# The forgetting term of the attention scores, from four-row matmuls to matmuls over all 128 rows

## The reference

```
log_f  = log_sigmoid(fc + b_f)              # 512 frames x 4 heads
F      = cumsum(log_f, over frames)
logits = (q @ k.T) * 64**-0.5 + F[query] - F[key]   # per head
p      = softmax(logits where key <= query)
out    = p @ v
```

## Time and profile before

| | us |
|---|---|
| median of 3 runs (lowest to highest) | 1547.85 (1547.56 to 1548.93) |
| the profiled execution, its own time | 1548.7 |
| its span | 1546.9 |
| TensorE matmuls busy | 1521.0 (98%) |
| VectorE busy | 1013.9 (66%) |
| ScalarE busy | 703.6 (45%) |

### The profile page before, as it was taken

How to read it: one execution, slowest core, us unless ns; L and a number is a source line. 1 busy time by engine, 2 the same in 40 slices (tenths; PEclk the granted TensorE clock), 3 DMA queues, 4 the chain that set the end, 5 groups by cost and what they waited for, 6 DMA issues and landing times.

```text
span 1546.9 us, 20345 instructions
## 1 busy us (share of the span) xinstructions
PE 1521.0 (98%) x7184; PEld 1232.9 (80%) x7184; DVE 1013.9 (66%) x1818; ACT 703.6 (45%) x1214; POOL 49.9 (3%) x39
## 2 busy tenths in 40 slices
PE   7899999999999999999999999999999999999997
PEld 5677877788888888888877788777888888888886
DVE  5778765556587743777468787655656777357754
ACT  5666554433444422443376565433434443234434
POOL 0000000000300000000110000000021000000011
PEclk9999999999999999999999999999999999999999
DMA  6222212223232223332432112122323332333232
GB/s 225 69 68 69 69 62 69 68 87 111 86 105 95 86 92 113 98 102 68 124 122 82 67 57 80 57 69 75 94 84 118 98 104 73 104 109 96 80 92 74
DMA packets 43862, 139.27 MB, mean 90 GB/s; under 512 B 5508, under 2 KB 5636, under 8 KB 43528
## 3 DMA queue, kind: packets, MB, share of 16 engines
q1 hardware_dynamic: 43344, 137.45, 28.3%
q10 hardware_dynamic: 440, 0.80, 0.2%
HBM read 136.13 MB, written 2.10 MB: 89 GB/s over the span
## 4 chain that ended last, share of the span: by engine, by line
PE 92%; DVE 3%; ACT 3%; issue 1%; DMA 0%; SPq 0%; DVEq 0%; ACTq 0%
PE dense L565 28%; PE dense L567 27%; PE dense L566 27%; PE branch L625 2%; PE turned L610 2%; PE scores L596 1%; PE scores L597 1%; PE scores L600 1%; ACT tmp L919 1%; DVE wlo L1066 0%; DMA h<-in_x 0%; ACT whi L792 0%; DVE act L1146 0%; DVE act L1143 0%; PE dense L778 0%
## 5 line engine op out<-in xcount | busy, mean ns | idle before, releaser
L565 PE MATMUL dense<-hg,whi 128*128 128x512 f32 x1376 | 552.2, 401 | 13.4 <-DVE wlo L1080 9.0
L567 PE MATMUL dense<-hg,wlo 128*128 128x512 f32 x1376 | 538.8, 392 | 0.0
L566 PE MATMUL dense<-hg,whi 128*128 128x512 f32 x1376 | 538.2, 391 | 0.0
L792 ACT ACTIVATE whi<-raw 128x1024 fp32r<-128x1024 f32 (+3 forms) x275 | 266.6, 969 | 451.6 <-PE dense L567 450.7
L1066 DVE TENSOR_TENSOR wlo<-raw,whi 128x1024 fp32r<-128x1024 f32 (+3 forms) x275 | 306.7, 1115 | 169.6 <-ACT whi L792 166.5
L565 PEld LDWEIGHTS dense<-hg,whi 128*128 128x128 f32 x1376 | 259.8, 189 | 76.8 <-issue 10.7
L567 PEld LDWEIGHTS dense<-hg,wlo 128*128 128x128 f32 x1376 | 259.4, 189 | 55.9
L566 PEld LDWEIGHTS dense<-hg,whi 128*128 128x128 f32 x1376 | 260.0, 189 | 50.6 <-issue 0.7
L565 PE MATMUL dense<-act,whi 128*128 128x512 f32 x608 | 239.2, 393 | 0.0
L567 PE MATMUL dense<-act,wlo 128*128 128x512 f32 x608 | 236.8, 390 | 0.0
L566 PE MATMUL dense<-act,whi 128*128 128x512 f32 x608 | 236.7, 389 | 0.0
(11 more groups left out here) (136 smaller groups left out, 1240.6 us busy)
## 6 DMA issues: line engine op xcount, KB each, us to landing
raw<-in_w_up SPq DMA_DIRECT2D x88, 512.0 KB, 3.5
raw<-in_w_gate SPq DMA_DIRECT2D x48, 512.0 KB, 3.5
raw<-in_w_in SPq DMA_DIRECT2D x35, 512.0 KB, 3.5
raw<-in_w_down SPq DMA_DIRECT2D x32, 384.0 KB, 3.0
raw<-in_w_down SPq DMA_DIRECT2D x32, 320.0 KB, 2.9
raw<-in_w_out SPq DMA_DIRECT2D x16, 512.0 KB, 3.5
raw<-in_w_br_a SPq DMA_DIRECT2D x8, 512.0 KB, 3.5
h<-in_x SPq DMA_DIRECT2D x8, 256.0 KB, 6.6
```

The costliest lines, as they stand in the source:

```text
L565: mm(out, a, xhi, start=start, stop=False)
L566: mm(out, a, xlo, start=False, stop=False)
L567: return mm(out, b, xhi, start=False, stop=stop)
L792: fn(whi[:, s, 0:cols], raw[:, r, 0:cols], ACT.Copy).then_inc(w_hi.sem, 1)
```

## The change

`f_rows` is replaced by two tiles. `fk` (128 x 512) is the key's side as before, all heads in one tile. `fq` (128 x 4 x 512) is the query's side, once for each head f: the sum of before, multiplied by `own_rows[:, f]`, which is 1 on rows 32f to 32f+31 and 0 elsewhere. The third matmul of a C step takes all 128 rows of both. So ahead of unit 15 VectorE has five instructions where it had two: four for `fq` (with two operands that are columns) and one for `fk`. The constants grow by four columns, and the program is built with `dynamic_dma_scratch_size=1024`.

```diff
+    parts["own_rows"] = np.arange(P)[:, None] // 32 == np.arange(4)[None, :]
...
-                  ("spread1", 2), ("eps", 1)):
+                  ("spread1", 2), ("own_rows", 4), ("eps", 1)):
...
-        f_rows = sb("f_rows", [P, 2, S], F32R)
+        fq = sb("fq", [P, 4, S], F32R)
+        fk = sb("fk", [P, S], F32R)
...
                 if forget:
-                    f = 32 * (2 * (p - A_PAIRS - B_PAIRS) + s)
-                    last = mm(b[:, 0:n], f_rows[f:f + 4, 0, t * P:(t + 1) * P], f_rows[f:f + 4, 1, 0:n],
-                              start=False, stop=True)
+                    f = 2 * (p - A_PAIRS - B_PAIRS) + s
+                    last = mm(b[:, 0:n], fq[:, f, t * P:(t + 1) * P], fk[:, 0:n], start=False, stop=True)
...
                         dve.wait_ge(group.sem, group.at(l, c))
-                        ve.tensor_scalar(f_rows[:, c, :], bank[g % 4][:, :], spread1[:, c:c + 1], None,
-                                         ALU.add).then_inc(aug.sem, 1)
+                        if c == 0:
+                            for f in range(4):
+                                last = ve.tensor_scalar(fq[:, f, :], bank[g % 4][:, :], spread1[:, 0:1],
+                                                        own_rows[:, f:f + 1], ALU.add, ALU.mult)
+                        else:
+                            last = ve.tensor_scalar(fk[:, :], bank[g % 4][:, :], spread1[:, 1:2], None, ALU.add)
+                        last.then_inc(aug.sem, 1)
...
-    nc = bacc.Bacc("TRN2", target_bir_lowering=False, num_devices=1)
+    nc = bacc.Bacc("TRN2", target_bir_lowering=False, num_devices=1, dynamic_dma_scratch_size=1024)
```

More of the change, by code:

```diff
@@ L269, in build @@
         mask_a, mask_b, mask_c = const("mask_a"), const("mask_b"), const("mask_c")
-        spread1, eps = const("spread1"), const("eps")
+        spread1, own_rows, eps = const("spread1"), const("own_rows"), const("eps")
         gains = sb("gains", [P, (2 * L + 1) * C])
```

## The result

| | before | after |
|---|---|---|
| median, us | 1548.17 | 1537.77 |
| lowest to highest | 1547.56 to 1548.93 | 1537.38 to 1538.03 |
| the profiled execution, its own time | 1548.7 | 1538.03 |
| its span | 1546.9 | 1536.2 |

The median is 10.4 us lower: the ratio is 0.9932, 95% interval 0.9919 to 0.9944 (four runs each). The median forecast was 1538.3, the range 1536.4 to 1541.7.

A forecast was written before the change was run, and what follows sets the result against it. TensorE, busy for 98% of the span, was taken to bound the kernel. A gain of 10.6 us and a VectorE cost of 1.0 made -9.6 us, from a median of 1547.85 to 1538.3 us; range 1536.4 to 1541.7.

The forecast's parts named there:

- The gain: In the 32 C steps, the third score matmul loses a fixed price of 0.33 us each, 10.6 us in all.
- The cause, the passage: TensorE pays 0.33 us for passing between four-row and 128-row matmuls and back in each C step, not for four rows.
- The spreading matmuls: Four-row matmuls starting 0.23 and 0.24 us apart among themselves, with 0.31 to the next over 128 rows; evidence for the passage.
- The load at nothing: The third matmul's 128-row weight load, 188 ns, stays hidden under the matmul before; exposed, it would return 6.0 us.
- Rival 2: The third matmul's weight load is exposed on TensorE, giving back 6.0 us: 1544.3 us; chance 0.03.
- The cost: VectorE's three further instructions make it 2.1 us late per layer; 0.3 and 0.7 us reach TensorE, 1.0 in all.
- the 0.30 us that are left: Layer 0: of VectorE's 2.1 us lateness, pauses take up 1.80; the rest reaches TensorE at the scores opening B's first pair.
- the signs: Marks expected in the timelines after, among them a possible wait for ScalarE's copy some steps after `fq`.
- The edits at nothing: Later `aug`, the bank held 2.1 us longer, four more constant columns and the DMA scratch: no cost, half a microsecond allowed.
- The base: Profiled execution 1548.7 us, giving 1539.1 after the change; it stands 0.85 us above the three runs' median, 1547.85.
- Rival 1: The third matmul's fixed 0.33 us comes from taking other tiles, not from its rows; no gain, 1548.9 us; chance 0.05.
- rival 3: VectorE's four `fq` instructions run slower, eating the gain at 1.90 us each; 1552.7 us at 2.5 each; chance 0.05.

The follow-up runs named there:

- e1 to e4: Third matmul over 32 rows on the kernel before: 1547.95 us; over 100, 64 and 4 rows on the kernel after: 1538.22, 1549.30 and 1549.68 us.
- e9: The kernel after with the masked query tiles made later by GpSimd, and the spreading matmuls over all 128 rows too: 1536.27 us.
- e8: The kernel after with VectorE's four instructions for `fq` done twice, one group after the other: 1545.71 us.
- e10_after_again: The kernel after, unchanged, run again beside the kernel before on the same chip: 1538.26 us, ratio 0.9935.
- e4: The kernel after with the third matmul over four rows again, keeping the new tiles and VectorE's added work: 1549.68 us.

## Why the prediction was right

**The gain, 32 x 0.33 = 10.6 us:** right, and 5% too small. Measured: 11.1, 0.347 us a step. Each rounding went down (0.45 - 0.12 from starts given to 0.01 us); the step of 256 columns fell by 0.35, not 0.33. The long step fits as well: 1.16 us before, 0.82 after. The reading that carried it was to compare two whole steps and not two durations: line 600's own gaps before and behind would have given 0.28, and the last 0.06 lay in the transposes.

**The cause, the passage:** shown by e1 to e4. The spreading matmuls, the prediction's witness, were read from their second start on: their first gap, 0.34 us, is part of the passage and not of "the rate of any 512-column matmul" (e9). What the prediction had only from them holds in the disputed place with the tiles kept and the rows changed alone. It said "between four and 128"; the measured border lies between 64 and 100.

**The load at nothing:** right. 188 ns are hidden under a start distance of 0.12 us, for line 602 as for 598. The rule that a load overlaps only where the row group differs (the Trainium skill, "TensorE: Matmul & The Clock Gate", Part 3, The mechanism) does not hold for these loads over all rows. The same section also lets a load run ahead when it goes to a background weight buffer, which the 0.12 us would fit; no run here shows the buffer. Rival 2 falls.

**The cost, 0.3 + 0.7 = 1.0 us:** right in sum (1.05), and wrong in one place. The step that failed reads "So the 0.30 us that are left reach TensorE there", at B's first scores. In layer 0 nothing was left there: its wait is as long as before. The 0.35 us came earlier, at 135 us. VectorE's lateness delayed ScalarE's exponential of one step. Behind it in ScalarE's order stood a piece of the next queries (line 877) and then the copy of the transposed probabilities of an older step, and the next transposes wait for that copy, because they write the bank that it reads (`p_t` in `step_turn`). ScalarE's timeline:

```profile
133.67 0.29 ACT L887 ACTIVATE sink_e<-small,nmx 128x1 f32<-128x1 f32 x1 [2.37 <-DVE nmx L1171]
...
134.77 0.36 ACT L895 ACTIVATE probT<-turned 128x256 f32<-128x256 f32 x1
```

TensorE's:

```profile
134.85 0.28 PE L599 MATMUL scores<-act 128*128 128x256 f32 x1
135.28 0.41 PE L611 MATMUL turned<-consts,prob 128*128 128x128 f32 x2
```

The transposes start 0.43 us after the second score matmul instead of 0.12. In the kernel before ScalarE had sat idle for 0.74 us ahead of the same copy:

```profile
134.44 0.38 ACT L894 ACTIVATE probT<-turned 128x256 f32<-128x256 f32 x1 [0.74 <-PE branch L625]
```

I had counted the pauses of VectorE and not the order of ScalarE; the signs named a wait for ScalarE's copy as possible, but the sum gave it no price. In layer 1 the same stall comes (0.30), and the wait at B's first scores after it (0.31). e8, which makes the stall longer, has the wait for the copy by name, 1.34 us at 139.93. The price of one instruction (0.70) was 0.74 in a row. As a way to the amount, lateness less VectorE's pauses did better than as a way to the place: it gives 2.2 - 1.80 = 0.4 and 2.2 - 1.42 = 0.8 against 0.35 and 0.70 measured, and for e8, 5.2 us late, 3.4 and 3.8 against 3.5 and 4.7, so it fails in layer 1 there.

**The edits at nothing:** the constants, `aug`, the bank and the DMA scratch: TensorE has no wait at any of them, and the feed-forward stretches keep their length to 0.1 us, as the prediction demanded.

**The base:** the profiled execution was 1.06 us ahead of that of before when attention began, from a start-up that varies between runs. Without it, it would have taken 1538.03 + 1.06 = 1539.1, the 1539.1 forecast. That it fits to 0.1 us is luck: two small errors, 0.5 us too little gain and the end's 0.3 that no term stood for, nearly cancel. The medians fell by 10.4 us where 9.6 was forecast, and by 10.0 when the kernel after ran again (e10_after_again, 1538.26 against 1548.24); start-up and end differ by more than that between executions, so the medians can't say which term the 0.4 to 0.8 belong to.

Rival 1 fell by e4, rival 3 by 0.74 us an instruction where 1.90 would have decided.

## What to carry to other kernels

A small matmul between large ones is priced by its neighbours: with 64 rows or fewer between matmuls over 128 it cost 0.35 us beyond its columns, so filling its other rows with zeros paid here, where the zeros cost 1.05 us in all and 32 such places gave 11.1. The opposite holds for columns where two narrow matmuls run side by side: making them wide took more than the passage gave back. Read such a price between the starts of two otherwise equal stretches, long enough to hold the work behind it; and when an engine is made late, follow its consumer's whole queue, since what stalls may be an older piece of work that stands behind the late one.

## What the runs showed that I had not expected

- The border between the classes: 64 rows pay the full price (0.94 us), 100 rows none (0.60).
- A second column as an operand costs VectorE 54 ns in a pass of 512 columns (802 against 748 ns).
- Beside GpSimd's multiplications VectorE's normalisation of 256 columns took 0.78 us instead of 0.35, while the maximum of 128 columns behind it kept its length (0.29 us).
- The values' product takes 0.05 us an instruction over 64 columns, where the two heads' matmuls start in pairs, and 0.11 over 128.
- At a passage between the classes the weight load starts with its own matmul; without one it starts 0.11 us ahead of it.
